# Two of x's eight transposed pieces: by TensorE, or by transposing DMAs with GpSimd's copies

## The chip, the cores and the metric

The kernel runs on one core of one Trainium2 chip. The metric is the device time of one execution in microseconds. The time before is 2468.52 us, the median of three runs (2468.34 to 2468.70).

## What is computed

Two transformer blocks of width 2048 run one after the other on one sequence of 256 tokens, all in f32. Only the very start of the first block matters here:

```
h    = rmsnorm(x, norm_attn)            # x is 256 x 2048
proj = h @ w_in                         # w_in is 2048 x 6144; q, k, v of two attentions
```

Everything behind it (two attentions, the output projection, a gated FFN, then a second block with a forgetting attention, an mLSTM, gates and a convolved FFN) is computed by the same kernel and is not touched.

## The kernel before, in words

**Products.** TensorE contracts over partitions, so `x` (tokens on partitions) has to be turned: `xT` has the 2048 features in 16 tiles (kt) of 128 partitions by 256 tokens. Each f32 operand is kept as a rounded part and a rest (`xT_hi`, `xT_lo`, `w_hi`, `w_lo`), and each product is three matmuls: hi by hi (line 623), hi by w_lo (624), lo by w_hi (625). The row norm's factor is applied later, when the sums leave PSUM.

**Units.** All the work on weights is one long series of units. A unit is 256 rows of a weight (two kt) by 512 columns: 12 matmuls of TensorE. SyncE's queue loads its 512 KB into `raw[n % 4]`, ScalarE makes `w_hi` (line 1042), VectorE makes `w_lo` (line 1449). There are four slots, so SyncE loads unit n when VectorE has split unit n - 4 (`lo_ready`), and ScalarE splits unit n + 4 when TensorE is done with unit n (`slot_used`). SyncE issues its loads one by one, in the order of the program: in stage `in_b`, three loads for each of units 1 to 7, four for each of units 8 to 15 (lines 502 and 505).

**The start.** The first group of 512 columns of stage `in_b` walks over all 16 kt in units 0 to 7, unit u needing kt 2u and 2u + 1. x comes in eight pieces of 256 columns, 256 KB each (`load_x`, line 444; pieces 6 and 7 are issued behind the weight loads of units 5 and 6). Piece j holds kt 2j and 2j + 1. For each piece:

- TensorE transposes its four 128x128 blocks into a PSUM bank (`start_T`, line 755; `start_more` waits for the piece and for the bank) and raises `kt_T`. Pieces 2 to 7 are turned behind units 0 to 5 (`behind` at line 826).
- ScalarE writes two tiles of `xT_hi` (`start_tile`, line 1066) and raises `kt_hi`; VectorE writes two tiles of `xT_lo` (`start_tiles`, line 1468) and raises `kt_lo`. For pieces 4 to 7 they do so right behind splitting the weights of units 4 to 7.
- TensorE waits ahead of unit u for `kt_lo` to reach 2u + 2 (`tiles_ready`, line 706).

Each engine works in the order of its program, so a wait in it holds all that stands behind it. ScalarE also sums squares of x for the norm (`half_squares`, line 1079), behind units' splits 1 to 4; GpSimd makes the norm's factor of them (line 2016 on), and before that it issues 14 small transfers (line 2007) and is then idle.

**The other way of turning, already used.** From the first attention head on, q and k (and much else) are turned without TensorE. A DMA can transpose 2-byte elements only, so GpSimd copies the f32 words apart into low and high halves (`halve_qk`, line 2049), SyncE issues a transposing DMA of 256 KB (`turn_heads`, line 454, at the units in `QK_ASKED`), and GpSimd joins the halves again into `qkT` (`join_turned`, line 2054). The same buffers serve this: `qk_bufs[1]`, `p_bufs[1]` and `qkT`, which are not in use during the first eight units.

Of the kernel before, what the change touches and what calls it, by code (L numbers as in the profile page):

```python
# [23 lines left out]
ACT = mybir.ActivationFunctionType  # L24
X = mybir.AxisListType.X
U16 = mybir.dt.uint16

P = 128
D = 2048
S = 256  # L30
NT = S // P
KT = D // P
# [14 lines left out]
NS = 4  # L47
# [13 lines left out]
G_ATTN, G_FFN, G_FINAL, G_NORM1, G_NORM2 = (KT * j for j in range(5))  # L61
# [53 lines left out]
START_BANKS = (4, 5, 6, 7, 2, 3, 4, 5)  # L115
# [57 lines left out]
            if 0 <= unit - HEAD_FIRST - k * HEAD_EVERY <= DIFF_STEPS[-1]]  # L173


QK_ASKED = {HEAD_FIRST + k_ * HEAD_EVERY + QK_SENT: k_ for k_ in range(2 * HEADS)}
QK_ASKED.update({PH["in_f"][0] + h_ * MLSTM_EVERY + 5: 2 * HEADS + h_ for h_ in range(M_HEADS)})
QK_ASKED.update({PH["gate_m"][0] + 12 * h_ + (4 if h_ else 6): 2 * HEADS + M_HEADS + h_ for h_ in range(4)})
QK_ASKED.update({PH["gate_a"][0] + 8 * h_ + (5 if h_ else 4): 2 * HEADS + M_HEADS + 4 + h_ for h_ in range(4)})
P_ASKED = {HEAD_FIRST + k_ * HEAD_EVERY + P_SENT: k_ for k_ in range(2 * HEADS)}  # L180
# [81 lines left out]
def two_blocks(nc, a, out):  # L262
    ctx = ExitStack()
    with ctx:
        def sb(name, shape, dt=F32):
            return ctx.enter_context(nc.sbuf_tensor(name, [P, *shape], dt))

        def sem(name):
            return ctx.enter_context(nc.semaphore(name))


        x = sb("x", [NT, D])
        xT_hi, xT_lo = sb("xT_hi", [KT * S], F32R), sb("xT_lo", [KT * S], F32R)
# [11 lines left out]
        gain = sb("gain", [N_GAIN])  # L285
# [20 lines left out]
        qkT = sb("qkT", [2, S])  # L306
# [21 lines left out]
        ps = [ctx.enter_context(nc.psum_tensor(f"ps{j}", [P, W], F32)) for j in range(8)]  # L328
# [21 lines left out]
        def across_bufs(buf, flipped_buf=None):  # L350
# [3 lines left out]
        qk_bufs = [across_bufs(z2[:, 0, C3 // 2:C3 // 2 + 4 * S]), across_bufs(z1[:, 0, 0:4 * S]),  # L354
                   across_bufs(tables), across_bufs(z2[:, 1, HALF:HALF + 2 * S], z2[:, 1, 2 * HALF:2 * HALF + 2 * S])]
        p_bufs = [across_bufs(z2[:, 1, C3 // 2:C3 // 2 + 4 * S]), across_bufs(z1[:, 1, 0:4 * S])]
        causal_bufs = [(split_[:, 0:3 * P].bitcast(U16).rearrange("p (e n) -> p e n", e=2), to[:, 0:3 * P].bitcast(U16).rearrange("p (e f s) -> p e f s", e=2, f=3))
                       for split_, to in ((work[:, 10 * S:12 * S], spare), *((z1f[:, c:c + 3 * P], z1f[:, c + 3 * P:c + 6 * P]) for c in (NT * (D + W), NT * D)))]
        y_split, y_flipped = (z2[:, 0, C3 - 2 * S + c * S:C3 - S + c * S].bitcast(U16).rearrange("p (t e n) -> p t e n", t=NT, e=2) for c in range(2))
        y_turned = z2[:, 1, C3 - 2 * S:C3 - S]  # L360
        qkT_halves = qkT[:, :, :].rearrange("p c s -> p (c s)").bitcast(U16).rearrange("p (f t s e) -> p f t s e", f=2, t=NT, e=2)
# [14 lines left out]
        x_landed = [sem(f"x_landed{j}") for j in range(4)]  # L376
# [4 lines left out]
        kt_T, kt_hi, kt_lo = sem("kt_T"), sem("kt_hi"), sem("kt_lo")  # L381
# [7 lines left out]
        halved, across, x_turned = sem("z_halved"), sem("z_across"), sem("x_turned")  # L389
        y_halved, y_across = sem("diff_y_halved"), sem("diff_y_across")  # L390
        m_halved, fox_joined = sem("mlstm_halved"), sem("fox_joined")
        qk_halved, qk_across, p_halved, p_across = sem("qk_halved"), sem("qk_across"), sem("p_halved"), sem("p_across")
        tanh_ready, silu_step, act_hi, act_lo = sem("tanh_ready"), sem("silu_step"), sem("act_hi"), sem("act_lo")
        conv_start, conv_step = sem("conv_start"), sem("conv_step")
# [40 lines left out]
        def _(sp):  # L435
# [9 lines left out]

            def turn_heads(unit):

                if unit in QK_ASKED:
                    k = QK_ASKED[unit]
                    sp.wait_ge(qk_halved, k + 1)  # L450
                    if 2 * HEADS <= k < 2 * HEADS + M_HEADS:
                        sp.wait_ge(m_halved, k + 1 - 2 * HEADS)
                    split_, flipped_ = qk_bufs[qk_buf(k)]
                    sp.dma_start_transpose(flipped_.rearrange("p t e f s -> p (t e f) s"),
                                           split_.rearrange("p t e n -> p (t e n)")).then_inc(qk_across, 16)
                if unit in Y_ASKED:
                    sp.wait_ge(y_halved, Y_ASKED[unit] + 1)
                    sp.dma_start_transpose(y_flipped.rearrange("p t e s -> p (t e) s"), y_split.rearrange("p t e n -> p (t e n)"))\
                      .then_inc(y_across, 16)
                if unit in P_ASKED:  # L460
                    k = P_ASKED[unit]
                    sp.wait_ge(p_halved, k + 1)
                    if k < 2 * HEADS:
                        split_, flipped_ = p_bufs[p_buf(k)]
                        to, of = flipped_.rearrange("p t e f s -> p (t e f) s"), split_.rearrange("p t e n -> p (t e n)")
                    else:
                        split_, flipped_ = causal_bufs[p_buf(k) - 2]
                        to, of = flipped_.rearrange("p e f s -> p (e f) s"), split_.rearrange("p e n -> p (e n)")
                    sp.dma_start_transpose(to, of).then_inc(p_across, 16)
# [100 lines left out]
            for i in range(2):  # L570
                for j in range(8):
                    n = PH["out_b"][0] + j
                    src, c = rows(w_out, HALF, D)[j % 4], (2 * i + j // 4) * W
# [42 lines left out]
        def _(pe):  # L616
# [207 lines left out]


            def behind(u):
                if u < 6:
                    start_more(2 + u)
                if u == 8:
                    small_T()  # L830
                if u in (10, 11):
                    pe.wait_ge(gain_ready, u - 8)
                heads(u)
# [196 lines left out]
        def _(act):  # L1030
# [31 lines left out]
            def start_tile(kt):  # L1062
                act.wait_ge(kt_T, kt // 2 + 1)
                if kt == 0:
                    act.wait_ge(gain_ready, 1)
                nc.scalar.activation(xT_hi[:, kt * S:(kt + 1) * S], ps[START_BANKS[kt // 2]][:, kt % 2 * S:(kt % 2 + 1) * S],
                                     ACT.Copy, scale=gain[:, G_ATTN + kt:G_ATTN + kt + 1]).then_inc(kt_hi, 1)
            for u in range(NS):
                if u == 1:
                    split(u, None, 0)  # L1070
# [5 lines left out]
            def half_squares(t, half):  # L1076

                c = slice(half * (D // 2), (half + 1) * (D // 2))
                nc.scalar.activation(sq_out0[:, t, c], x[:, t, c], ACT.Square, accum_out=half_ss[:, half, t:t + 1]).then_inc(x_sq, 1)
# [62 lines left out]
                        evac(name, i, g, z, (2 * i + g) * W, W, rstd)  # L1142

            def behind(u):
                if u < NS:
                    start_tile(2 * (NS + u))
                    start_tile(2 * (NS + u) + 1)
                if u in (1, 2):
                    half_squares(u - 1, 0)
                if u in (3, 4):  # L1150
                    half_squares(u - 3, 1)
                if u == 6:
                    act.wait_ge(rstd_ready, 1)
                if u == 9:
                    act.wait_ge(lam_step, 2)
                    nc.scalar.activation(lam_t[:, 2:4], lam_t[:, 0:2], ACT.Exp).then_inc(lam_exp, 1)
                heads_out(u, "in_b", 0, z1)
                heads(u)
# [281 lines left out]
        def _(dve):  # L1440
            v = nc.vector
# [22 lines left out]
            def start_tiles(u):  # L1464
                for kt in (2 * u, 2 * u + 1):
                    dve.wait_ge(kt_hi, 2 * u + 2)
                    c = slice(kt * S, (kt + 1) * S)
                    v.scalar_tensor_tensor(xT_lo[:, c], ps[START_BANKS[kt // 2]][:, kt % 2 * S:(kt % 2 + 1) * S],
                                           gain[:, G_ATTN + kt:G_ATTN + kt + 1], f32(xT_hi[:, c]), ALU.mult, ALU.subtract).then_inc(kt_lo, 1)
            dve.wait_ge(first_landed, 32)  # L1470
            v.tensor_copy(w_hi[0][:, 0, :], raw[0][:, 0, :]).then_inc(first_hi, 1)
# [105 lines left out]
                    (diff_head, dil_head)[kind](u, Head(0, head, 0))  # L1577

            def behind(u):
                if u < NS:  # L1580
                    start_tiles(NS + u)
                if u == 8:
                    parameters()
                if u == 9:
                    more_parameters()
                heads(u)
# [392 lines left out]
        def _(pool):  # L1979
            g_ = nc.gpsimd  # L1980
# [29 lines left out]
            def factor(n, dst):  # L2010
# [2 lines left out]
                pool.wait_ge(ms_ready, n)  # L2013
                return g_.tensor_tensor(dst[:], ms[:], minus_half[:, 0:NT], ALU.pow)

            pool.wait_ge(x_sq, 4)
            g_.tensor_tensor(ss[:], half_ss[:, 0, :], half_ss[:, 1, :], ALU.add).then_inc(x_sq, 1)
            pool.wait_ge(x_sq, 5)
# [37 lines left out]
            def join_qk(k):  # L2056

                s, head = (hb, ha)[k // HEADS], k % HEADS
                pool.wait_ge(hb.scores, 2 * min(k, HEADS))
                if k > HEADS:  # L2060
                    pool.wait_ge(ha.scores, head)
                join_turned(k).then_inc(s.qkT, 1)
# [284 lines left out]
```

## Time and profile before

| what | value |
|---|---|
| median of three runs | 2468.52 us (2468.34 to 2468.70) |
| the profiled execution's own time | 2468.15 us |
| its span in the profile | 2466.4 us |
| TensorE busy | 2460.6 us, 10974 matmuls |
| VectorE busy | 1497.7 us |
| ScalarE busy | 1208.0 us |
| GpSimd busy | 620.8 us |
| granted clock of TensorE | 1.0 over the span |

The span is the stretch between the first and the last instruction of the core; 1.75 us of the execution's time lie around it. Busy times of the engines overlap. In the rows below, L623 is line 623 of the kernel, PE is TensorE, PEld its weight loads, ACT ScalarE, DVE VectorE, POOL GpSimd and SPq the queue on which SyncE issues DMAs. Positions are microseconds from the span's start. A landing is counted from the start of the DMA's issue.

### The profile page before, as it was taken

To read this page: it belongs to the slowest core of one execution; us is meant where nothing else is said; L and a number is where in the kernel's file an instruction comes from. 1 tells how busy PE (TensorE), PEld (TensorE's weight loads), DVE (VectorE), ACT (ScalarE), POOL (GpSimd) and SP (SyncE) were. 2 spreads that over 40 slices of the span, in tenths; PEclk is the share of its full clock that TensorE was granted. 3 is DMA by queue.
4 is the path that set the end of the run, shared out by engine and by line. 5 is a ranking of instruction groups with operands and counts; after the bars stand their busy time and mean duration, and the time that the engine had idled before them with its cause. 6 is when DMAs were issued, how large, how long until landed. Compare 5 with 4: busy or idle time off the path is not lost.

```text
span 2466.4 us, 30149 instructions
## 1 busy us (share of the span) xinstructions
PE 2460.6 (100%) x10974; PEld 2037.7 (83%) x10974; DVE 1497.7 (61%) x1724; ACT 1208.0 (49%) x1622; POOL 620.8 (25%) x537
## 2 busy tenths in 40 slices
PE   9999999999999999999999999999999999999999
PEld 7888888888888888888888888888888888888887
DVE  5776666555455555565455555676567646675665
ACT  6555445444344434455444544544555545553553
POOL 2665524210012100131012322332334103320230
PEclk9999999999999999999999999999999999999999
DMA  9888868776677667687666677777777767876775
GB/s 251 214 204 213 207 195 228 210 204 201 192 204 208 202 195 201 201 242 205 177 205 201 191 204 202 209 214 223 220 217 203 219 192 220 219 208 195 202 227 178
DMA packets 491609, 511.80 MB, mean 208 GB/s; under 512 B 187136, under 2 KB 290020, under 8 KB 491360
## 3 DMA queue, kind: packets, MB, share of 16 engines
q1 hardware_dynamic: 489312, 507.36, 73.3%
q0 software_dynamic: 1088, 2.07, 0.3%
q8 instruction: 73, 1.20, 0.2%
q10 hardware_dynamic: 1088, 0.79, 0.1%
q14 instruction: 48, 0.39, 0.1%
HBM read 467.38 MB, written 2.11 MB: 190 GB/s over the span
## 4 chain that ended last, share of the span: by engine, by line
PE 99%; DMA 0%; ACT 0%; ACTq 0%; DVE 0%; issue 0%
PE ps L623 32%; PE ps L625 32%; PE ps L624 32%; PE ps L718 0%; PE ps L733 0%; PE ps L786 0%; PE ps L799 0%; DMA x<-in_x 0%; PE ps L975 0%; PE ps L755 0%; PE ps L658 0%; PE ps L952 0%; PE ps L907 0%; PE ps L906 0%; PE ps L640 0%; PE ps L645 0%
## 5 line engine op out<-in xcount | busy, mean ns | idle before, releaser
L1449 DVE TENSOR_TENSOR w_lo<-raw,w_hi 128x1024 fp32r<-128x1024 f32 x880 | 1152.2, 1312 | 921.8 <-ACT w_hi L1042 919.0
L1042 ACT ACTIVATE w_hi<-raw 128x1024 fp32r<-128x1024 f32 x879 | 929.4, 1059 | 1141.5 <-PE ps L625 1080.5
L623 PE MATMUL ps<-w_hi,xT_hi 128*128 128x512 f32 x2196 | 859.8, 392 | 0.0
L625 PE MATMUL ps<-w_hi,xT_lo 128*128 128x512 f32 x2196 | 854.9, 389 | 0.0
L624 PE MATMUL ps<-w_lo,xT_hi 128*128 128x512 f32 x2196 | 854.6, 389 | 0.0
L623 PE MATMUL ps<-w_hi,yT_hi 128*128 128x512 f32 x1312 | 511.0, 390 | 0.0
L625 PE MATMUL ps<-w_hi,yT_lo 128*128 128x512 f32 x1312 | 510.4, 389 | 0.0
L624 PE MATMUL ps<-w_lo,yT_hi 128*128 128x512 f32 x1312 | 510.4, 389 | 0.0
L623 PEld LDWEIGHTS ps<-w_hi,xT_hi 128*128 128x128 f32 x2196 | 412.3, 188 | 88.0 <-issue 2.5
L625 PEld LDWEIGHTS ps<-w_hi,xT_lo 128*128 128x128 f32 x2196 | 412.3, 188 | 85.8
L624 PEld LDWEIGHTS ps<-w_lo,xT_hi 128*128 128x128 f32 x2196 | 412.4, 188 | 85.0
L2138 POOL COPY work<-z 128x1024 uint16<-128x1024 uint16 x98 | 168.4, 1746 | 1046.7 <-DVE z L1679 543.2
L624 PEld LDWEIGHTS ps<-w_lo,yT_hi 128*128 128x128 f32 x1312 | 246.3, 188 | 51.1
L625 PEld LDWEIGHTS ps<-w_hi,yT_lo 128*128 128x128 f32 x1312 | 246.3, 188 | 51.1
L623 PEld LDWEIGHTS ps<-w_hi,yT_hi 128*128 128x128 f32 x1312 | 246.3, 188 | 50.9
L2143 POOL COPY work<-work 128x1024 uint16<-128x1024 uint16 x98 | 152.1, 1581 | 196.5 <-DMA work<-work 177.7
L1896 DVE SCALAR_TENSOR_TENSOR z<-work,conv,z 128x255 f32<-128x255 f32 (+1 forms) x176 | 74.7, 483 | 0.6
L1089 ACT ACTIVATE z<-ps,rstd 128x512 f32<-128x512 f32 x86 | 53.7, 675 | 0.0
L1391 ACT ACTIVATE z<-work,conv 128x256 f32<-128x256 f32 x88 | 45.4, 587 | 0.0
L2054 POOL COPY qkT<-z 128x1024 uint16<-128x1024 uint16 x20 | 29.6, 1479 | 36.7 <-DMA z<-z 36.7
L2068 POOL COPY z<-work 128x1024 uint16<-128x1024 uint16 x16 | 25.4, 1587 | 46.0 <-DVE work L1520 30.1
L1179 ACT ACTIVATE junk<-z 128x512 f32<-128x512 f32 x24 | 15.2, 635 | 31.4 <-DVE z L1628 31.0
(215 smaller groups left out, 924.7 us busy)
## 6 DMA issues: line engine op xcount, KB each, us to landing
raw<-in_w_up SPq DMA_DIRECT2D x264, 512.0 KB, 4.3
raw<-in_w_down SPq DMA_DIRECT2D x176, 512.0 KB, 4.4
raw<-in_w_in SPq DMA_DIRECT2D x160, 512.0 KB, 4.3
raw<-in_w_gate SPq DMA_DIRECT2D x88, 512.0 KB, 4.5
raw<-in_w_out SPq DMA_DIRECT2D x60, 512.0 KB, 4.6
raw<-in_w_in SPq DMA_DIRECT2D x191, 128.0 KB, 2.7
raw<-in_w_in SPq DMA_DIRECT2D x127, 192.0 KB, 3.1
raw<-in_w_proj_m SPq DMA_DIRECT2D x16, 512.0 KB, 4.0
```

What stands on the lines that cost most here:

```text
L623: pe.matmul(o, hi[:, q], w_hi[n % NS][:, k, 0:width], start=first, stop=False)
L624: pe.matmul(o, hi[:, q], w_lo[n % NS][:, k, 0:width], start=False, stop=False)
L625: mm = pe.matmul(o, lo[:, q], w_hi[n % NS][:, k, 0:width], start=False, stop=last)
L1042: nc.scalar.activation(w_hi[n % NS][:, :, 0:width], raw[n % NS][:, :, 0:width], ACT.Copy).then_inc(hi_ready, 1)
L1089: nc.scalar.activation(o, pair[g][t][:, 0:width], func, scale=scale[:, t:t + 1]).then_inc(by_act, 1)
L1391: nc.scalar.activation(z[:, f, :], turned[:, f, :], ACT.Identity, scale=conv[:, ds(col + 2 * CONV_T, 1)], bias=conv[:, ds(col + 3 * CONV_T ...
L1449: v.tensor_tensor(w_lo[n % NS][:, :, 0:width], raw[n % NS][:, :, 0:width], f32(w_hi[n % NS][:, :, 0:width]), ALU.subtract).then_inc(lo_rea ...
L1896: v.scalar_tensor_tensor(z[:, f, j:S], turned[:, f, 0:S - j], w, z[:, f, j:S], ALU.mult, ALU.add).then_inc(conv_step, 1)
L2054: return g_.tensor_copy(qkT_halves, qk_bufs[qk_buf(k)][1].rearrange("p t e f s -> p f t s e"))
L2068: g_.tensor_copy(p_bufs[k // HEADS][0], (mix_halves, prob_halves)[k // HEADS]).then_inc(p_halved, 1)
L2138: g_.tensor_copy(halves[:, t, :, :], z[:, t, :].bitcast(U16).rearrange("p (n e) -> p e n", e=2)).then_inc(halved, 1)
L2143: return g_.tensor_copy(turned_halves[:, c, :], flipped.rearrange("p e f s -> p (f s) e")[:, c, :])
```

## The change

Pieces 6 and 7 (`X_TURNED` = 6) go the other way:

- GpSimd waits for the two pieces and halves each into one buffer (`x_halved`), at the place where it otherwise waited for the sums of squares.
- SyncE issues the first transposing DMA behind the weight loads of unit 7 and the second behind those of unit 9 (`X_ASKED`). Ahead of the first it waits for the halving; ahead of the second also for `kt_T` 7, so for the first join.
- GpSimd joins piece 6 into `qkT` and raises `kt_T` to 7; then it joins piece 7 into the same `qkT`, when VectorE has read piece 6 out of it (`kt_lo` 14), and raises `kt_T` to 8.
- ScalarE and VectorE read these pieces from `qkT` in place of PSUM, and one unit later than before: piece 6 behind the split of unit 7, piece 7 behind that of unit 8. Pieces 4 and 5 keep their places.
- TensorE no longer transposes pieces 6 and 7 behind units 4 and 5.

```diff
+X_TURNED, X_ASKED = 6, {7: 0, 9: 1}
...
+        x_bufs = (qk_bufs[1], p_bufs[1])
...
             def turn_heads(unit):
 
+                if unit in X_ASKED:
+                    k = X_ASKED[unit]
+                    sp.wait_ge(x_halved, k + 1)
+                    if k:
+                        sp.wait_ge(kt_T, X_TURNED + k)
+                    split_, flipped_ = x_bufs[k]
+                    sp.dma_start_transpose(flipped_.rearrange("p t e f s -> p (t e f) s"),
+                                           split_.rearrange("p t e n -> p (t e n)")).then_inc(x_across, 16)
...
             def behind(u):
-                if u < 6:
+                if 2 + u < X_TURNED:
                     start_more(2 + u)
...
-                nc.scalar.activation(xT_hi[:, kt * S:(kt + 1) * S], ps[START_BANKS[kt // 2]][:, kt % 2 * S:(kt % 2 + 1) * S],
-                                     ACT.Copy, scale=gain[:, G_ATTN + kt:G_ATTN + kt + 1]).then_inc(kt_hi, 1)
+                src = ps[START_BANKS[kt // 2]][:, kt % 2 * S:(kt % 2 + 1) * S] if kt // 2 < X_TURNED else qkT[:, kt % 2, :]
+                nc.scalar.activation(xT_hi[:, kt * S:(kt + 1) * S], src, ACT.Copy, scale=gain[:, G_ATTN + kt:G_ATTN + kt + 1]).then_inc(kt_hi, 1)
...
             def behind(u):
-                if u < NS:
-                    start_tile(2 * (NS + u))
-                    start_tile(2 * (NS + u) + 1)
+                if u in (0, 1, 3, 4):
+                    j = NS + u - u // 3
+                    start_tile(2 * j)
+                    start_tile(2 * j + 1)
                 if u in (1, 2):
                     half_squares(u - 1, 0)
+                if u == 3:
+                    act.wait_ge(x_landed[2], 32)
+                    act.wait_ge(x_landed[3], 32)
...
-                if u < NS:
-                    start_tiles(NS + u)
+                if u in (0, 1, 3, 4):
+                    start_tiles(NS + u - u // 3)
...
+            for k in range(KT // 2 - X_TURNED):
+                j = X_TURNED + k
+                pool.wait_ge(x_landed[j % 4], 16 * (j // 4 + 1))
+                g_.tensor_copy(x_bufs[k][0], x[:, :, j * 2 * P:(j + 1) * 2 * P].bitcast(U16).rearrange("p t (n e) -> p t e n", e=2)).then_inc(x_halved, 1)
+            for k in range(KT // 2 - X_TURNED):
+                j = X_TURNED + k
+                pool.wait_ge(x_across, 16 * (k + 1))
+                pool.wait_ge(kt_T, j)
+                if k:
+                    pool.wait_ge(kt_lo, 2 * j)
+                g_.tensor_copy(qkT_halves, x_bufs[k][1].rearrange("p t e f s -> p f t s e")).then_inc(kt_T, 1)
             pool.wait_ge(x_sq, 4)
...
+                if k == 0:
+                    pool.wait_ge(kt_lo, KT)
```

VectorE's source in `start_tiles` (line 1468) changes as ScalarE's does. The last wait stands in `join_qk` (line 2056), ahead of the first head's join.

## Rows read from the trace of the kernel before

**Rows 1.** Page: busy time, chain by engine, ScalarE's weight splits (busy, mean | idle before)

```profile
PE 2460.6 (100%) x10974; PEld 2037.7 (83%) x10974; DVE 1497.7 (61%) x1724; ACT 1208.0 (49%) x1622; POOL 620.8 (25%) x537
...
PE 99%; DMA 0%; ACT 0%; ACTq 0%; DVE 0%; issue 0%
...
L1042 ACT ACTIVATE w_hi<-raw 128x1024 fp32r<-128x1024 f32 x879 | 929.4, 1059 | 1141.5 <-PE ps L625 1080.5
```

**Rows 2.** Waits of TensorE in the whole span: total us, times, longest

```profile
PE ps L766 <- POOL ones L1981: 1.1, 1, 1.1
PE ps L755 <- DMA x<-in_x: 0.7, 1, 0.7
PE ps L640 <- DVE w_hi L1471: 0.6, 1, 0.6
```

**Rows 3.** Timeline of TensorE, 17 to 31: start us, us, engine, line, operation

```profile
23.68 0.60 PE L755 MATMUL ps<-ident,x 128*128 128x128 f32 x4
24.03 0.48 PE L623 MATMUL ps<-w_hi,xT_hi 128*128 128x512 f32 x1
...
26.88 0.60 PE L755 MATMUL ps<-ident,x 128*128 128x128 f32 x4
27.23 0.48 PE L623 MATMUL ps<-w_hi,xT_hi 128*128 128x512 f32 x1
...
30.08 0.40 PE L623 MATMUL ps<-w_hi,xT_hi 128*128 128x512 f32 x1
```

**Rows 4.** Timeline of ScalarE, 14 to 36

```profile
26.77 1.06 ACT L1042 ACTIVATE w_hi<-raw 128x1024 fp32r<-128x1024 f32 x1 [0.57 <-DMA raw<-in_w_in]
27.73 0.82 ACT L1066 ACTIVATE xT_hi<-ps,gain 128x256 fp32r<-128x256 f32 x2
```

**Rows 5.** Timeline of VectorE, 14 to 33

```profile
27.86 1.23 DVE L1449 TENSOR_TENSOR w_lo<-raw,w_hi 128x1024 fp32r<-128x1024 f32 x1 [1.79 <-ACT w_hi L1042]
29.00 0.87 DVE L1468 SCALAR_TENSOR_TENSOR xT_lo<-ps,gain,xT_hi 128x256 fp32r<-128x256 f32 x2
```

**Rows 6.** Timeline of SyncE's queue, 14 to 36

```profile
14.34 0.46 SPq L444 DMA_DIRECT2D x<-in_x  x1
...
19.83 1.22 SPq L502 DMA_DIRECT2D raw<-in_w_in  x1
21.09 15.20 SPq L505 DMA_DIRECT2D raw<-in_w_in  x25
```

**Rows 7.** Line 444, 14.3 to 14.4: the load of piece 6, issue to landing

```profile
DMA to landing us min/median/max: 7.0/7.0/7.0
```

**Rows 8.** Line 505, 21.1 to 22.8: four weight loads (unit 8) and their landing

```profile
L505 SPq DMA_DIRECT2D raw<-in_w_in x4: 468/474/689, 21.1 to 22.6; - x4
...
DMA to landing us min/median/max: 4.3/4.4/5.9
```

**Rows 9.** Line 502, 19.7 to 20: unit 7's last load, issue to landing

```profile
DMA to landing us min/median/max: 6.9/6.9/6.9
```

**Rows 10.** Line 454 in the whole span: 256 KB transposing DMAs and their landing

```profile
L454 SPq DMA_TRANSPOSE z<-z x20: 1231/1232/2064, 45.1 to 1588.4; - x20
...
DMA to landing us min/median/max: 3.1/4.3/7.4
```

**Rows 11.** Timeline of GpSimd, 0 to 45: last small transfer and the next work

```profile
15.46 0.55 POOL L2007 DMA_DIRECT2D z<-in_conv_b  x1
31.72 0.19 POOL L2017 TENSOR_TENSOR ss<-half_ss 128x2 f32<-128x2 f32 x1 [15.72 <-ACT z L1079]
```

**Rows 12.** Lines 2049 and 2054: GpSimd's halving and joining copies; ns min/median/max

```profile
L2049 POOL COPY z<-work x16: 1036/1036/2015, 39.1 to 311.4; 128x1024 uint16<-128x1024 uint16 x16
...
L2054 POOL COPY qkT<-z x16: 1155/1298/2177, 48.7 to 321.5; 128x1024 uint16<-128x1024 uint16 x16
```

**Rows 13.** Timeline of TensorE, 0 to 12: the matmuls of ones

```profile
1.05 2.93 PE L766 MATMUL ps<-ones 128*128 128x128 f32 x12 [1.05 <-POOL ones L1981]
...
4.75 1.06 PE L766 MATMUL ps<-ones 128*128 128x128 f32 x8
```

More of the change, by code:

```diff
@@ L391, in two_blocks @@
         m_halved, fox_joined = sem("mlstm_halved"), sem("fox_joined")
+        x_halved, x_across = sem("x_halved"), sem("x_across")
         qk_halved, qk_across, p_halved, p_across = sem("qk_halved"), sem("qk_across"), sem("p_halved"), sem("p_across")
@@ L1467, in start_tiles @@
                     c = slice(kt * S, (kt + 1) * S)
-                    v.scalar_tensor_tensor(xT_lo[:, c], ps[START_BANKS[kt // 2]][:, kt % 2 * S:(kt % 2 + 1) * S],
+                    src = ps[START_BANKS[u]][:, kt % 2 * S:(kt % 2 + 1) * S] if u < X_TURNED else qkT[:, kt % 2, :]
+                    v.scalar_tensor_tensor(xT_lo[:, c], src,
                                            gain[:, G_ATTN + kt:G_ATTN + kt + 1], f32(xT_hi[:, c]), ALU.mult, ALU.subtract).then_inc(kt_lo, 1)
```

## The prediction, made before the changed kernel was run

> **What bounds the kernel now.** I read the page first: TensorE is busy 2460.6 us of the span of 2466.4, the chain that ended last is 99% TensorE, and ScalarE's splitting of the weights sits idle for over 1000 us waiting for TensorE [rows 1]. So weights are ahead, and nearly every microsecond that TensorE gains or loses is gained or lost for good. The waits of TensorE say whether a loss could be taken up later: they are three, 2.4 us in all, none behind the first ten microseconds [rows 2]. There is no slack behind the start. 0.2% of this time, 4.9 us, is about what a measurement of this kernel can tell from no change. Then I read the timelines of the five engines over the first 36 us, since the edit touches nothing else.
>
> **What it removes.** Two groups of four transposes leave TensorE. Unit 5 with the group behind it takes 27.23 - 24.03 = 3.20 us, unit 6 without one 30.08 - 27.23 = 2.85 [rows 3]: 0.35 each, 0.7 together. That is all that the edit can give, if everything else stays hidden: 2468.15 - 0.7 = 2467.45. Without these groups unit 5 would start at 24.03 - 0.35 = 23.68, unit 6 could start at 26.5, unit 7 at 29.4.
>
> **Where the tiles stand in ScalarE's and VectorE's order.** Piece 6 now comes behind the split of unit 7. That split waits for its weights and starts at 26.77; the two tiles behind it take 27.73 to 28.55 [rows 4]. VectorE splits unit 7 from 27.86 and does the two tiles from 29.00 to 29.87 [rows 5]. In the kernel before these places held piece 7, which unit 7 needs at 30.08, so they cost nothing. Now they hold piece 6, which unit 6 needs at 26.5. So even with piece 6 turned in time, unit 6 starts at 29.9: TensorE stands still for 3.4 us. Unit 7 could then start at 29.9 + 2.85 = 32.75, 2.7 us later than the 30.08 of before. This part is nearly certain.
>
> **Piece 6 on its way.** Its load is issued at 14.34 [rows 6] and lands 7.0 us later [rows 7], at 21.35. GpSimd is free by then: its last small transfer ends at 16.0 and it sat idle for 15.7 us until 31.72 [rows 11]. The halving isn't in the trace; its nearest row is the same copy for q and k, 1.04 us at the least and 2.0 at most [rows 12]. I take 1.2, since VectorE works beside it: 22.55. SyncE has issued unit 7's last load by 21.05 [rows 6], so its queue stands for 1.5 us. The issue itself holds the queue for 1.23 us [rows 10], until 23.8. The landing takes 3.1 to 7.4 us, in the median 4.3 [rows 10]; weight loads issued at 21 to 23 took 4.3 to 5.9 [rows 8]. I take 4.3, so 26.85; the join is 1.16 to 2.2, I take 1.3 [rows 12]: `kt_T` 7 stands at 28.15. ScalarE's place at 27.73 thus slips by 0.4, to 28.15 to 29.0, VectorE's tiles end about 29.9, and unit 6 starts at 30.0. Twenty transposing DMAs of a whole piece's size landed within 7.4 us each [rows 10]. The Trainium skill speaks against the edit: VectorE: DVE Perf Modes, The three transpose paths, gives a 128x128 transpose of 2-byte elements 390 ns on TensorE and 1309 ns by DMA, and tells to use TensorE where PSUM will do as the destination. A piece is eight such blocks; by that page, one after the other, they would be an estimated 10.5 us of DMA, and the two pieces would move the end by some 13 us more than my sum. The trace doesn't agree with eight in a row, so this gets no chance of its own.
>
> **Piece 7 on its way.** It is issued at 23.8 + the loads of units 8 and 9. These are eight issues; the queue's rate in rows is 0.47 to 0.69 us each when nothing holds it [rows 8], and 15.20 / 25 = 0.61 over a stretch with its waits [rows 6]. I take 0.55, so 28.2, which meets the other condition, `kt_T` 7 at 28.15. Issue at 28.2; by then the queue has been thin for a while, so I take the landing at 3.7, between the least and the median [rows 10]: 31.9. The join waits for `kt_lo` 14 (29.9, passed) and ends at 33.2. ScalarE's two tiles take 0.82 [rows 4], VectorE's 0.87 [rows 5], one behind the other since VectorE waits for both of ScalarE's: 34.9. Seven hand-overs of about 0.04 (unit 7's last load lands at 19.83 + 6.9 = 26.73 and its split starts at 26.77; VectorE follows ScalarE's end at 27.83 by 0.03 [rows 4, 5, 6, 9]) and rounding make 35.3. Unit 7 starts at 35.3 where it started at 30.08: **+5.2 us**. Halving of piece 7 lies in GpSimd's wait for the DMA and costs nothing; piece 7's load is issued ahead of unit 7's last, at 19.83 [rows 6], so with the same 7.0 it lands by 26.8 and is halved by 28.0.
>
> **What is queued behind the new waits.** On ScalarE, stuck ahead of piece 7's tiles: the last half of the squares and the splits of unit 9 on. Unit 9's split then ends at about 34.2 + 1.1 + 1.1 = 36.4, VectorE's at 37.7; TensorE wants unit 8 at 38.1 and unit 9 at 41, both are ready. On SyncE: two issues (2.5 us) and a stand of 1.5 us ahead of all loads from unit 8 on; unit 8's weights land near 30 and are split by 33. TensorE moves later by more than the queue does, so no load becomes late. On GpSimd: the norm's factor, wanted by ScalarE ahead of its first emptying of PSUM, which waits for unit 7 anyhow. I cost these at nothing; their cover is TensorE's own lateness.
>
> **The sum.** The own time of the profiled execution is 2468.15, 0.37 under the median. With +5.2 it is 2473.35, and against the median 2473.7 us, 0.21% more. The bounds of the unknown prices: with every one at its least (halving 1.04, issues of 0.49, landing 3.1, join 1.16) unit 7 starts at 33.8, +3.7; with halving 2.0, landings of 5.9 and 4.3, joins of 1.8 it is 39.2, +9.1.
>
> **The rivals.**
> 1. *Not slower by 0.2%.* SyncE's queue is the place: if halving, issue, eight loads, landing and join together take less than the 11.8 us that I gave them by 0.3 or more, the shift is under 4.9, down to 3.7, or 2.7 where only the order counts. For it: the least prices are near what an unhurried queue shows; against it: loads issued around 21 to 23 took 4.3 us and more [rows 8]. Time 2471.2 to 2473.4, about 2472.7. Chance 0.36.
> 2. *The clock falls.* TensorE stands for 3.5 us, works for 2.85, stands for 2.4. Its first 12 matmuls of ones took 2.93 us (0.24 each, the level of 1.2 GHz), the next eight 1.06 (0.13, the level of 2.4) [rows 13]; nothing in the trace stands so long behind that. If it falls, unit 6 takes 5.7, ends at 35.7, 0.4 past unit 7's tiles, and unit 7 may lose up to 2.85 in turn: +5.6 to +8.5, some 2475.5. Chance 0.10. The Trainium skill (TensorE: Matmul & The Clock Gate, Part 1) says that an idle TensorE falls back to half its rate and has to work to get it back, which is this rival.
> 3. *A late landing.* The first transposing DMA shares the queue's backlog: unit 7's last load took 6.9 us [rows 9]. With landings of 6 to 7 us `kt_T` 7 is late, the second issue waits for it, and the shift is +7 to +9: 2476.5. Chance 0.09.
> 4. *All hidden.* The gain of 0.7 stays, 2467.8. Against it stands the order on ScalarE; it needs unit 7's weights to land 3.4 us sooner than in the trace. Chance 0.02.
>
> **How the numbers follow.** The forecast, a shift of 4.9 to 7 by waiting for the second piece, has 0.43; it and rivals 2 and 3 are slower by over 0.2%: 0.62 less 0.01 for prices at the edge, 0.61. Rivals 1 and 4 are within 0.2%: 0.38. Faster by over 0.2% has no mechanism here; 0.01 is kept for what I overlook. The range goes from 2471.2, where the order alone counts, to 2478.0, the upper bound of the sum with a little of the clock's. The forecast's own range is 2473.4 to 2475.5.
>
> **What would show it.** In the changed kernel's timeline of TensorE: no line 755 behind unit 3; a stand from 26.5 to about 30 ahead of unit 6, released by VectorE's tile; another from 32.8 to about 35.3 ahead of unit 7; then no wait at all, and the total of waits up by 5 to 6 us. On SyncE a stand at 21.05 until 22.6. GpSimd: halvings at 21.4 and from about 24, joins ending near 28.2 and 33.3. I am wrong if unit 6 starts ahead of 29, if the second issue goes out well away from 28.2, if matmuls of unit 6 are 0.46 apart, or if the shift at unit 7 is right and the end differs.

## The result, and the profile after

The changed kernel takes **2474.29 us** in the median of 11 runs (2473.76 to 2475.07), the kernel before beside it 2468.38 (2468.07 to 2468.70, 11 runs): +5.9 us, a ratio of 1.0024 with a 95% interval of 1.0016 to 1.0032. The profiled execution is the run of 2475.07; it is compared with the 2468.15 of the profiled one before, +6.9. The rows come in the order of [rows 1 to 12].

The page, and below it the waits of TensorE (total, times, longest), changed kernel:

```profile
PE 2462.1 (100%) x10966; PEld 2037.8 (82%) x10966; DVE 1500.5 (61%) x1724; ACT 1208.4 (49%) x1622; POOL 631.6 (26%) x541
...
PE 98%; DMA 1%; SPq 1%; POOL 0%; issue 0%; DVE 0%; ACT 0%; POOLq 0%
```

```profile
PE ps L634 <- DVE xT_lo L1484: 4.4, 3, 3.6
PE ps L766 <- DMA x<-in_x: 1.7, 1, 1.7
PE ps L777 <- POOL ones L1997: 1.1, 1, 1.1
```

TensorE has eight matmuls fewer and is yet busy for 1.5 us more [rows 1]: something ran slowly. The second wait is for piece 1 and grew by 1.0 by chance (0.7 in [rows 2]; 0.7 to 1.3 in most profiles below). The first is new.

TensorE's timeline:

```profile
27.72 0.39 PE L636 MATMUL ps<-w_hi,xT_lo 128*128 128x512 f32 x1
31.66 0.80 PE L634 MATMUL ps<-w_hi,xT_hi 128*128 128x512 f32 x1 [3.56 <-DVE xT_lo L1484]
32.25 0.63 PE L635 MATMUL ps<-w_lo,xT_hi 128*128 128x512 f32 x1
32.68 0.63 PE L636 MATMUL ps<-w_hi,xT_lo 128*128 128x512 f32 x1
...
35.35 0.40 PE L634 MATMUL ps<-w_hi,xT_hi 128*128 128x512 f32 x1
35.59 0.40 PE L635 MATMUL ps<-w_lo,xT_hi 128*128 128x512 f32 x1
...
36.86 0.50 PE L634 MATMUL ps<-w_hi,xT_hi 128*128 128x512 f32 x1 [0.66 <-DVE xT_lo L1484]
```

Unit 6 starts at 31.66 after a stand of 3.56. Its first matmuls are 0.43 us apart, the last ones 0.24: TensorE's clock had fallen, and came back inside the unit. Unit 7 starts at 36.86 where it started at 30.08 [rows 3], 6.8 later. The windows of the same kernel show the clock (the column behind POOL's busy time is the granted share of full speed; 0.50 is 1.2 GHz):

```profile
28.00:32.00 4.00, 0.45 (x2) 0.34 (x2) 1.63 (x3) 2.21 (x5) 1.75 (x1) 0.94 0.90 222
32.00:36.00 4.00, 4.00 (x12) 2.97 (x11) 1.30 (x2) 1.69 (x4) 1.95 (x1) 0.63 0.88 228
36.00:50.00 14.00, 13.34 (x62) 10.89 (x62) 9.12 (x19) 8.32 (x11) 5.12 (x9) 1.00 0.72 207
```

The way of the two pieces, which [rows 4 to 6, 11] answer to: GpSimd, SyncE's queue, ScalarE and VectorE, one timeline each.

```profile
22.13 1.03 POOL L2035 COPY z<-x 128x1024 uint16<-128x1024 uint16 x1 [6.06 <-DMA x<-in_x]
24.98 1.04 POOL L2035 COPY z<-x 128x1024 uint16<-128x1024 uint16 x1 [1.82 <-DMA x<-in_x]
27.54 2.21 POOL L2042 COPY qkT<-z 128x1024 uint16<-128x1024 uint16 x1 [1.52 <-DMA z<-z]
33.01 1.95 POOL L2042 COPY qkT<-z 128x1024 uint16<-128x1024 uint16 x1 [3.25 <-DMA z<-z]
```

```profile
21.03 0.84 SPq L513 DMA_DIRECT2D raw<-in_w_in  x1
23.19 1.64 SPq L457 DMA_TRANSPOSE z<-z  x1
24.88 4.16 SPq L516 DMA_DIRECT2D raw<-in_w_in  x8
29.84 1.24 SPq L457 DMA_TRANSPOSE z<-z  x1
```

```profile
29.79 0.91 ACT L1078 ACTIVATE xT_hi<-qkT,gain 128x256 fp32r<-128x256 f32 x2 [2.30 <-POOL qkT L2042]
34.99 0.91 ACT L1078 ACTIVATE xT_hi<-qkT,gain 128x256 fp32r<-128x256 f32 x2 [2.31 <-POOL qkT L2042]
```

```profile
22.19 2.06 DVE L1464 TENSOR_TENSOR w_lo<-raw,w_hi 128x1024 fp32r<-128x1024 f32 x1 [1.76 <-ACT w_hi L1053]
27.52 1.23 DVE L1464 TENSOR_TENSOR w_lo<-raw,w_hi 128x1024 fp32r<-128x1024 f32 x1 [0.42 <-ACT w_hi L1053]
35.93 0.88 DVE L1484 SCALAR_TENSOR_TENSOR xT_lo<-qkT,gain,xT_hi 128x256 fp32r<-128x256 f32 x2 [1.99 <-ACT xT_hi L1078]
```

Line 457, the first and the second issue, to their landing:

```profile
DMA to landing us min/median/max: 4.3/4.3/4.3
...
DMA to landing us min/median/max: 3.1/3.1/3.1
```

Each hand-over is the one foretold: halving, issue, landing, join, `xT_hi`, `xT_lo`, unit. The join of piece 6 took 2.21 us. Ends are read off these rows by start plus duration: it ended at 29.75 and released the second issue at 29.84, though the queue had been free since 24.88 + 4.16 = 29.04.

### The profile page after: what moved, and what is told of

Its sections match the earlier page's. It is cut to its first block, busy times and chain, and to the rows that moved or that the text cites. A ratio compares the mean times of both kernels' runs of the same rounds, so it can differ in the third digit from the quotient of the medians.

```text
span 2473.3 us, 30141 instructions
## 1 busy us (share of the span) xinstructions
PE 2462.1 (100%) x10966; PEld 2037.8 (82%) x10966; DVE 1500.5 (61%) x1724; ACT 1208.4 (49%) x1622; POOL 631.6 (26%) x541
## 4 chain that ended last, share of the span: by engine, by line
PE 98%; DMA 1%; SPq 1%; POOL 0%; issue 0%; DVE 0%; ACT 0%; POOLq 0%
PE ps L634 32%; PE ps L636 32%; PE ps L635 32%; PE ps L729 0%; PE ps L744 0%; PE ps L797 0%; DMA z<-z 0%; PE ps L810 0%; DMA x<-in_x 0%; SPq L516 0%; PE ps L986 0%; SPq L513 0%; POOL qkT L2042 0%; PE ps L963 0%; SPq L447 0%; PE ps L918 0%
```

## The experiments

The kernels of one group ran on one chip, beside the kernel before; "+" is a median over that median. Beside it stands the profiled execution: where unit 7 starts, less the 30.08 of before, and its own time less 2468.15.

| kernel | median us | + | unit 7 | own time |
|---|---|---|---|---|
| again | 2474.35 | +6.0 | +6.9 | +7.1 |
| order_only | 2470.81 | +2.5 | +4.0 | +4.4 |
| gain_alone | 2468.16 | -0.2 | -0.2 | 0.0 |
| kept_busy | 2477.42 | +9.1 | +9.2 | +9.3 |
| kept_busy2 | 2474.29 | +5.8 | +6.4 | +6.6 |
| old_order | 2474.57 | +6.1 | +6.4 | +6.7 |
| side_work | 2469.49 | +1.0 | +0.9 | +1.8 |
| no_chain | 2472.88 | +4.4 | +5.9 | +6.2 |
| no_chain_busy | 2473.97 | +5.4 | +5.6 | +5.7 |
| join_alone | 2474.39 | +5.8 | +6.2 | +6.3 |
| no_chain_again | 2472.70 | +4.3 | +5.7 | +5.6 |
| no_chain_ones | 2472.23 | +3.9 | +3.9 | +4.0 |

(The kernel before had 2468.32 in the group of the first four, 2468.48 in that of kept_busy2 to no_chain, 2468.59 in that of the next two and 2468.38 in the last.) With one exception, side_work, a profiled run's own time moves by as much as the start of unit 7 does, within 0.4 us: what happens behind unit 7 adds little and gives nothing back. Where an expectation names a theory by a letter, the text below it says in words which held.

**again: the changed kernel, unaltered.**

> The changed kernel unaltered, as the measure for the others on the same chip. Theory A (TensorE waits for the tiles of piece 6 and then of piece 7): some 5.5 to 6 us above the kernel before, and in the profile a stand of 3 to 4 us ahead of unit 6 and a further one ahead of unit 7. In the first profile one microsecond of the 6.9 lay ahead of all this, in the landing of piece 1 (6.3 us where it had been 5.3). If that belongs to the change it is here again; if it is chance, unit 4 starts at the place it has in the kernel before and the shift is nearer 5.9.

2474.35 us (2473.40 to 2475.21, 10 runs), ratio 1.0024 (1.0015 to 1.0034): the result stands on another chip. All ten runs have a mean granted clock of 0.999, where the kernel before has 1.0 in 25 of its 26 (the other took 2470.68). In the profile here unit 6 took 5.2 us, from 31.79 to 36.97, and piece 7's tiles were done at 36.94: unit 7 followed at 36.99 without a wait.

**order_only: the kernel before, with the later places alone.** In ScalarE's program, and likewise in VectorE's:

```diff
-                if u < NS:
-                    start_tile(2 * (NS + u))
-                    start_tile(2 * (NS + u) + 1)
+                if u in (0, 1, 3, 4):
+                    j = NS + u - u // 3
+                    start_tile(2 * j)
+                    start_tile(2 * j + 1)
```

> The kernel before, with TensorE's transposes kept, and only the places of pieces 6 and 7 in ScalarE's and VectorE's order moved one unit later. Theory A: unit 6 can't start ahead of 29.9, unit 7 not ahead of 32.7, so the end is 2.7 us later (2.5 to 3.0), near 2471.1. Rival B (only the DMA route costs, the order lies in its shadow or costs nothing): within 0.3 us of the kernel before.

2470.81 us (2470.39 to 2472.50, 11 runs), ratio 1.0010 (1.0001 to 1.0019). TensorE's timeline and two windows of its profiled run, which is its slowest:

```profile
29.99 0.50 PE L623 MATMUL ps<-w_hi,xT_hi 128*128 128x512 f32 x1 [1.98 <-DVE xT_lo L1469]
...
31.50 0.63 PE L623 MATMUL ps<-w_hi,xT_hi 128*128 128x512 f32 x1
31.93 0.63 PE L624 MATMUL ps<-w_lo,xT_hi 128*128 128x512 f32 x1
...
34.49 0.57 PE L624 MATMUL ps<-w_lo,xT_hi 128*128 128x512 f32 x1
```

```profile
30.00:32.00 2.00, 2.00 (x8) 1.63 (x9) 1.36 (x2) 2.00 (x4) 0.00 (x0) 0.86 0.84 237
32.00:34.00 2.00, 2.00 (x6) 1.60 (x5) 1.30 (x3) 1.32 (x3) 1.11 (x3) 0.50 0.65 184
```

Unit 6 starts where the prediction had its floor, 29.9. The nine runs with a clock of 1.0 have a median of 2470.61, +2.3 where 2.7 was worked out. The two with 0.999 took 2472.13 and 2472.50, 1.7 more. So a stand of 2.0 us can bring the clock down, in some runs and not in others, and here nothing covers it.

**gain_alone: the removal, with nothing in its place.** TensorE leaves out the transposes of pieces 6 and 7 and no other engine makes them, so the last four kt of `xT` are made of what lies in those banks. ScalarE waits for the loads of those pieces itself.

```diff
-                if u < 6:
+                if u < 4:
                     start_more(2 + u)
...
-                act.wait_ge(kt_T, kt // 2 + 1)
+                act.wait_ge(kt_T, min(kt // 2 + 1, 6))
```

> The kernel before without the transposes of pieces 6 and 7 and with nothing in their place: ScalarE and VectorE read what is left in the banks, so the last four kt of xT are those of earlier pieces, and the output isn't the reference's. It gives the most that the change could have won. Theory A, from the rows: 0.7 us less than the kernel before (0.35 per group), 0.9 if the late first matmul behind each group counts too. Rival D (the transposes lay in a wait for weights or tiles): no difference.

2468.16 us (2467.74 to 2468.37, 11 runs), ratio 0.9998 (0.9989 to 1.0007): 0.16 gained, not 0.7, and the interval includes no change. TensorE's timeline shows where it went:

```profile
29.91 0.50 PE L623 MATMUL ps<-w_hi,xT_hi 128*128 128x512 f32 x1 [0.61 <-DVE xT_lo L1471]
```

Unit 7 waits 0.6 us for its tiles. VectorE starts them at 28.99 here and at 29.00 in [rows 5], whatever TensorE does, because they stand behind the split of unit 7's weights. In the kernel before they ended at 29.87, 0.2 ahead of unit 7. So the removal can give 0.2 at most, and this is the ceiling of the whole edit while the last tiles stand behind that split.

**kept_busy and kept_busy2: is the fall of the clock paid for?** Matmuls of ones ahead of units 6 and 7 of the changed kernel fill its stands; 30 and 14 in the first, 18 and 8 in the second.

```diff
+                if u in (5, 6):
+                    for _ in range((18, 8)[u - 5]):
+                        pe.matmul(ps[6][:, 0:P], ones[:], ones[:], start=True, stop=True)
                 if u == 8:
                     small_T()
```

> The changed kernel with 30 matmuls of ones (128 columns, result not read) ahead of unit 6 and 14 ahead of unit 7, so that TensorE doesn't stand and its clock shouldn't fall. In the changed kernel's profile seven matmuls of unit 6 were 0.43 us apart in place of 0.23, 1.4 to 1.6 us in all, and TensorE then still waited 0.66 us for piece 7. Theory A (the fall is covered, since unit 7 waits for piece 7's tiles anyhow): no shift against the changed kernel, within 0.4 us, and the stand ahead of unit 7 grows in place of the slow matmuls. Rival C (the clock is part of the loss): 1.3 to 1.6 us faster than the changed kernel.

> The changed kernel with fewer matmuls of ones than kept_busy, 18 ahead of unit 6 and 8 ahead of unit 7. A matmul of ones is two instructions of 0.113 us, so the 30 and 14 of kept_busy lasted 6.8 and 3.2 us, longer than the stands, and pushed unit 6 to 33.7; these last 4.1 and 1.8 us, shorter than the stands of 5.0 and (at full clock) 2.3. Theory A (the clock's fall is covered by the wait for piece 7): granted clock 1.0, unit 6 at full pace, and the end within 0.4 us of the changed kernel's 2474.35. Rival C (the fall is part of the loss): 1.3 to 1.6 us less, 2472.9.

kept_busy took 2477.42 us (2476.96 to 2478.38, 5 runs), ratio 1.0038 (1.0024 to 1.0051), and says nothing of the clock's price: I had sized it wrongly. Each call is two instructions of 0.11 us, so 30 of them lasted 6.9 us and held unit 6 themselves. kept_busy2, sized by that, took 2474.29 us (2474.07 to 2474.76, 10 runs), ratio 1.0023 (1.0013 to 1.0032), with a clock of 1.0 in every run. TensorE's timeline:

```profile
27.43 4.18 PE L842 MATMUL ps<-ones 128*128 128x128 f32 x36
...
34.19 1.95 PE L842 MATMUL ps<-ones 128*128 128x128 f32 x16
36.46 0.50 PE L634 MATMUL ps<-w_hi,xT_hi 128*128 128x512 f32 x1 [0.33 <-DVE xT_lo L1487]
```

With the clock kept up, unit 6 was done by 34.2 and unit 7 still waited for piece 7, until 36.46. The time is that of the changed kernel within 0.2 us. The clock falls in the changed kernel and costs nothing there that can be measured: the wait for piece 7 covers it, in the profile of again only just.

**old_order: the changed kernel with ScalarE's and VectorE's old places** (the diff of order_only, the other way round).

> The changed kernel with pieces 6 and 7 back at their old places in ScalarE's and VectorE's order, behind the splits of units 6 and 7. The order alone cost 2.3 us in runs whose clock stayed. Theory A says the two delays overlap and don't add: the join of piece 6 ends near 29.8, two microseconds behind ScalarE's later place, so the end stays within 0.5 us of the changed kernel's 2474.35. Rival E (they add): some 2.3 us less, 2472.0.

2474.57 us (2473.86 to 2476.12, 10 runs), ratio 1.0025 (1.0016 to 1.0034). Unit 6 started at 30.75, unit 7 at 36.51. Alone, the later places cost 2.3 us; taken out of the changed kernel they give nothing. The two delays lie beside one another.

**side_work: the kernel before, with the whole new route beside it, unused.** GpSimd, SyncE's queue and the DMAs do everything that the change gives them, the joined tiles are read by nobody, and TensorE's transposes serve.

```diff
+                if unit in X_ASKED:
+                    k = X_ASKED[unit]
+                    sp.wait_ge(x_halved, k + 1)
+                    if k:
+                        sp.wait_ge(x_joined, k)
...
+                g_.tensor_copy(qkT_halves, x_bufs[k][1].rearrange("p t e f s -> p f t s e")).then_inc(x_joined, 1)
```

> The kernel before, with TensorE's transposes and the old order in use, and beside it the whole new route run for nothing: halvings, both transposing DMAs at their places in SyncE's queue, both joins. It prices what is queued behind the new waits. Theory A: within 0.3 us of the kernel before, since weights are ahead by more than the 3 to 4 us by which the queue moves. Rival F: later weights or VectorE's splits, slowed beside GpSimd's copies (one took 2.1 us in place of 1.23 in the first profile), cost 0.5 to 2 us.

2469.49 us (2468.71 to 2469.94, 11 runs), ratio 1.0003 (0.9994 to 1.0012): +1.0. The interval includes no change, but even the fastest of these runs is above the median of the kernel before, 2468.48. Of the profiled run's +1.8, 0.6 stands ahead of the edit (TensorE starts piece 4's transposes at 17.63 where it did at 17.04). Some 0.3 more stands ahead of unit 7: VectorE's split of unit 7 took 2.16 us beside GpSimd's join (the rows are in the last section), so piece 7's tiles ended at 30.91 and the unit started at 30.98, where 0.23 behind its last matmul it would have been 30.67. ScalarE's and TensorE's timelines show what else:

```profile
35.71 1.06 ACT L1053 ACTIVATE w_hi<-raw 128x1024 fp32r<-128x1024 f32 x1 [2.40 <-DMA raw<-in_w_in]
38.02 1.06 ACT L1053 ACTIVATE w_hi<-raw 128x1024 fp32r<-128x1024 f32 x1 [1.25 <-DMA raw<-in_w_in]
...
42.60 1.06 ACT L1053 ACTIVATE w_hi<-raw 128x1024 fp32r<-128x1024 f32 x1 [1.42 <-DMA raw<-in_w_in]
```

```profile
43.11 0.50 PE L634 MATMUL ps<-w_hi,xT_hi 128*128 128x512 f32 x1 [0.48 <-DVE gain L1496]
```

The queue's two issues and their waits make the weights behind unit 7 late: ScalarE waits for their loads three times, where in the kernel before at most 0.66 us was waited for a load in that stretch. At 43.11 TensorE stands 0.5 us for VectorE's copy of later gains (`gain`), which stands in VectorE's order behind a split that is late with the loads. The other 0.4 of the 1.8 was not traced. The prediction put this at nothing, with TensorE's own lateness as the cover; with the cover gone the whole side work costs about 1.0.

**no_chain: the changed kernel, with the second transposing DMA asked for a unit sooner and joined into a buffer of its own**, so that it waits neither for the first join nor for VectorE.

```diff
-X_TURNED, X_ASKED = 6, {7: 0, 9: 1}
+X_TURNED, X_ASKED = 6, {7: 0, 8: 1}
...
-                    if k:
-                        sp.wait_ge(kt_T, X_TURNED + k)
...
-                if k:
-                    pool.wait_ge(kt_lo, 2 * j)
```

> The changed kernel without what makes piece 7 wait for piece 6: a second target buffer for the join and a semaphore of its own for the second DMA, which is asked behind the loads of unit 8 and waits for its halving alone. Its issue goes from 29.9 to about 27.1, piece 7's tiles from 37.0 to about 34.7. Theory A with the clock's fall: unit 6, started near 31.8 at half the clock, lasts until 36.1 to 36.9 and is now the bound itself, so the gain is 0 to 0.8 us: 2473.5 to 2474.3. Rival G (the clock is no bound): unit 7 starts at 34.7, 2.2 us less: 2472.2.

2472.88 us (2471.72 to 2474.33, 11 runs), ratio 1.0018 (1.0009 to 1.0027), 1.4 under kept_busy2 and 1.7 under old_order on the same chip, and between the two times expected (2473.5 to 2474.3 with the clock as the bound, 2472.2 without). The second issue went out at 27.30 and piece 7's tiles were ready at 34.0, but unit 7 started at 36.02: all of unit 6 ran at the lower clock. The cover of the clock's fall was gone. How much it costs was asked three times.

> no_chain with the 18 and 8 matmuls of ones of kept_busy2. In no_chain's profile piece 7's tiles were ready at 34.0, but unit 6 ran at half the clock from 30.73 and unit 7 started at 36.02. Theory A': the fall of the clock is covered while piece 7 comes late, and is the bound once it doesn't. Here unit 6 keeps its pace, the ones end near 35.3 at the latest, and the end is 0.8 to 1.6 us below no_chain's 2472.88, near 2471.7, where no_chain's one run with an undisturbed clock was. Rival H (the clock costs nothing here either): the same as no_chain within 0.4 us.

no_chain_busy has the 18 and 8 matmuls of ones of kept_busy2. 2473.97 us (2472.92 to 2474.72, 11 runs), where about 2471.7 was expected: a miss. Its tiles were ready at 34.6, but the second group of ones started at 34.02 and lasted 1.95, so it held unit 7 until 35.72. The next two ran side by side: no_chain unaltered, and no_chain with 18 matmuls of ones ahead of unit 6 alone.

> The version without the chain between the two pieces once more, unaltered, for a comparison on one chip with the next kernel. Both theories: about 1.5 us under the changed kernel, 4.4 above the kernel before; unit 6 runs at half pace all through and unit 7 starts near 36.0 although its tiles are ready near 34.0; granted clock 0.50 from 31 to 36.

> The same version with 18 matmuls of ones ahead of unit 6 alone and none ahead of unit 7, so that nothing added can hold unit 7. Theory A (without the wait for piece 7 as its cover, the fall of the clock costs real time): unit 6 starts near 31.2 at full pace, ends near 34.1, unit 7 starts with its tiles near 34.6, and the time is 1.0 to 1.5 us below the version without ones on the same chip. Theory G (the clock is not what holds the end there; the tiles and the later weights are): within 0.4 us of it. If the clock falls again in the short stand ahead of unit 7, the gain is smaller, 0.2 to 0.9, and the granted clock shows it from 34 on.

no_chain_again: 2472.70 us (2471.83 to 2473.97, 11 runs), ratio 1.0016 (1.0007 to 1.0025). no_chain_ones: 2472.23 (2471.34 to 2472.66, 11 runs), ratio 1.0015 (1.0006 to 1.0024). TensorE's timeline of no_chain_again, then of no_chain_ones:

```profile
30.75 0.80 PE L634 MATMUL ps<-w_hi,xT_hi 128*128 128x512 f32 x1 [4.23 <-DVE xT_lo L1484]
...
34.76 0.63 PE L634 MATMUL ps<-w_hi,xT_hi 128*128 128x512 f32 x1
...
35.73 0.39 PE L634 MATMUL ps<-w_hi,xT_hi 128*128 128x512 f32 x1
```

```profile
26.68 4.18 PE L842 MATMUL ps<-ones 128*128 128x128 f32 x36
30.79 0.50 PE L634 MATMUL ps<-w_hi,xT_hi 128*128 128x512 f32 x1
...
33.95 0.50 PE L634 MATMUL ps<-w_hi,xT_hi 128*128 128x512 f32 x1
```

Unit 6 starts at the same time in both, and unit 7 1.8 us earlier where the clock was kept up; the profiled runs differ by 2473.76 - 2472.11 = 1.65. The medians differ by only 0.5, where 1.0 to 1.5 was expected if the fall costs real time, and the two intervals overlap. The runs differ among themselves: the six of no_chain_again at 0.999 have a median of 2472.95, its five at 1.0 one of 2471.98, under the one with ones. So the fall costs 1.65 to 1.8 us where it hits in full and nothing covers it, by the two profiles, and some 0.5 in the median of this version, which is near the scatter of the runs.

**join_alone: the changed kernel, with VectorE's split of unit 7 behind piece 6's tiles**, so that nothing runs beside the join.

```diff
-            turn("in_b", 0, 16, behind)
+            for u in range(16):
+                if u == 3:
+                    behind(u)
+                split(NS + u, 0, 16)
+                if u != 3:
+                    behind(u)
```

> The changed kernel with one swap in VectorE's order: the split of unit 7 comes behind piece 6's tiles instead of ahead of them, so that it doesn't run beside GpSimd's first join. Where the two met, one of them took 2.1 to 2.2 us and the other its usual 1.15 or 1.23, in all profiles so far. Theory I (they share a way to the memory, and the join's length goes straight into the chain): first join 1.15 to 1.3 us, the split 1.23, both pieces 0.5 to 1 us earlier, the end 0.4 to 1.2 us below the changed kernel's 2474.35. Rival J (chance of the landings): joins as long as before and no change.

2474.39 us (2473.43 to 2476.05, 10 runs), ratio 1.0025 (1.0015 to 1.0034): no gain. GpSimd and the queue:

```profile
27.68 1.15 POOL L2047 COPY qkT<-z 128x1024 uint16<-128x1024 uint16 x1 [2.13 <-DMA z<-z]
33.18 1.15 POOL L2047 COPY qkT<-z 128x1024 uint16<-128x1024 uint16 x1 [4.35 <-DMA z<-z]
```

```profile
25.06 4.16 SPq L516 DMA_DIRECT2D raw<-in_w_in  x8
29.34 1.24 SPq L457 DMA_TRANSPOSE z<-z  x1
```

Both joins fell to 1.15 us, as the mechanism says, and the price I had given it was wrong. `kt_T` 7 now stood at 28.83, but the queue was busy with its eight loads until 29.22. The second issue left 0.5 us sooner than in the changed kernel, its landing took 3.8 instead of 3.1, and unit 7 started at 36.25. Behind the join stood the queue.

None of these versions beats the kernel before: the removal by itself gives 0.16 us, less than can be measured, and each way tried of making the two pieces elsewhere costs more. The old places together with no_chain's sooner second DMA were not tried.

## Why the prediction was right, and where its terms were off

The forecast held: slower by over 0.2%, by the wait for piece 7, inside the forecast's own range. Two of its own signs of being wrong showed all the same: the second issue went out 1.6 us later than foretold, and matmuls of unit 6 were 0.43 us apart. Term by term, against the profiled run of the changed kernel.

- **The removal, 0.7.** Over-valued: 0.16 (gain_alone). The step "unit 7 at 29.4" looked only at TensorE, and not at the tiles that end at 29.87 whatever it does. That row [rows 5] was in hand and used two paragraphs further down. Since the new waits hide it, the sum was not touched.
- **The order, a floor of 2.7.** Seen alone it is 2.3 (order_only), and in the changed kernel it doesn't bind: piece 6's own way ended later, so the old places give the same time (old_order). Right that the two are no sum.
- **Piece 6.** Landed and its halving begun at 22.13 (21.35 foretold; its issue was 0.8 late by the chance at the start), issue at 23.19 (22.55), of 1.64 us (1.23), landing 4.3 as foretold, join begun at 27.54 (26.85). Then the one step of the sum that was far off: the join at 1.3. It took **2.21**, so `kt_T` 7 stood at 29.75 and not at 28.15. The rows showed 1.16, a median of 1.3 and 2.2 [rows 12]; I took the median without asking what ran beside the long ones.
- **Piece 7.** Eight loads in 4.16 us, 0.52 each (0.55). Issue at 29.84 (28.2), landing 3.1 (3.7), join 1.95 (1.3), tiles and hand-overs 1.9 (2.1). Unit 7 at 36.86 (35.3), a shift of 6.8 for 5.2. The medians differ less, +5.9, since both profiled runs of this kernel were the slowest of theirs. Of the 0.7 that the median is over the forecast, join_alone shows that the join can't be all: without its delay the queue sets the same end.
- **The queue behind the waits, nothing.** Right with its cover, 1.0 without (side_work). Naming the cover was what made this testable.
- **The clock (rival 2).** Put at 0.10; it fell in all 21 runs of the changed kernel. The condition for its price was in the text: unit 6 at 5.7 us would end 0.4 past the tiles. But the clock came back inside the unit, so that it took 4.5 and ended at 36.2, under the cover; in the profile of again it took 5.2 and ended level with the tiles. That it cost nothing is in part luck: the cover had 0.6 us to spare in the one profile and nothing in the other. The chance of 0.10 for the fall was far too low. The Trainium skill (TensorE: Matmul & The Clock Gate, Part 1) says that an idle array falls to half its rate and must work to get it back; the trace agrees, with a granted clock of 0.63 from 32 to 36 and 1.00 from there on. What the prediction read off [rows 13] is a pace only: in the first 4 us of the kernel before the profile has a granted clock of 1.00, though the matmuls of ones are twice as far apart there.
- **A late landing (rival 3).** Not seen: 4.3 and 3.1 us for a whole piece, and 3.1 to 5.5 in all the profiles with this route. The Trainium skill (VectorE: DVE Perf Modes, The three transpose paths) has 1309 ns by DMA for a 128x128 block of 2-byte elements; by these rows, too, eight blocks are not turned one after the other at that figure, which would be an estimated 10.5 us.
- **Not slower by 0.2% (rival 1).** It was near: the interval of the ratio begins at 1.0016. no_chain, which takes one wait out of the chain, lies at 1.0018, under that bound.

## What to carry to other kernels

Ahead of taking work off the bounding engine, look at what comes ready next on the others: 0.7 us of TensorE was worth 0.16, since the next tiles stood 0.2 behind it. A route over another engine and a queue is a chain of hand-overs (here 7.6 us from piece 6's landing to `kt_T` 7, 22.13 to 29.75, for what TensorE does in 0.35), and shortening one link (the join, by 1.06 us) gives only what the link behind it leaves (0.5). A loss that is covered is not gone: the clock's fall and the side work behind the waits cost nothing in the changed kernel, and 0.5 to 1.8 us and about 1.0 where the cover was taken away.

## What the runs showed of the hardware

**GpSimd's copy and VectorE's split exclude one another.** Whichever of the two starts first runs at its own pace, and the other is held until it is done. Two pairs of the kernel side_work, GpSimd's timeline and then VectorE's:

```profile
27.89 1.17 POOL L2035 COPY qkT<-z 128x1024 uint16<-128x1024 uint16 x1 [2.41 <-DMA z<-z]
33.41 2.18 POOL L2035 COPY qkT<-z 128x1024 uint16<-128x1024 uint16 x1 [4.35 <-DMA z<-z]
```

```profile
27.97 2.16 DVE L1460 TENSOR_TENSOR w_lo<-raw,w_hi 128x1024 fp32r<-128x1024 f32 x1 [0.63 <-ACT w_hi L1053]
...
33.34 1.22 DVE L1460 TENSOR_TENSOR w_lo<-raw,w_hi 128x1024 fp32r<-128x1024 f32 x1 [1.07 <-ACT w_hi L1053]
```

First GpSimd is 0.08 ahead and VectorE takes 2.16 for what alone takes 1.23; then VectorE is 0.07 ahead and the join takes 2.18 for 1.15. Eighteen such pairs of a 128x1024 copy and a split, begun within 0.1 us of one another in the first 50 us of the profiles here, go the same way: eleven with GpSimd ahead (its copy 1.03 to 1.17, the split 2.04 to 2.22), seven with VectorE ahead (1.22 to 1.23, the copy 2.03 to 2.22). A few hundredths of a microsecond decide which engine pays about 1.0. The long copies of [rows 12] are such meetings too: of the 32 copies of the kernel before, the ten that took 1.4 us or more all began while VectorE ran a split, and the 22 of 1.04 to 1.16 did not. One of the ten, GpSimd's timeline and then VectorE's, kernel before:

```profile
221.91 2.02 POOL L2049 COPY z<-work 128x1024 uint16<-128x1024 uint16 x1
```

```profile
221.81 1.22 DVE L1449 TENSOR_TENSOR w_lo<-raw,w_hi 128x1024 fp32r<-128x1024 f32 x1 [1.36 <-ACT w_hi L1042]
```

The Trainium skill (SBUF — State Buffer, section "SBUF: two separate sides") says that a VectorE operation with two SBUF inputs and a GpSimd operation that reads SBUF share a pair of ports as an exclusive lock, the first to start keeping it for the whole instruction; the trace agrees in all eighteen, and join_alone, where its joins meet no split, has 1.15 twice.

**TensorE's clock falls in some runs and not in others of one kernel.** Behind a stand of 2.0 us it fell in 2 of 11 runs (order_only); with one of about 4.2 ahead of unit 6, 16 of the 22 runs of no_chain and no_chain_again show a mean of 0.999; with 3.6 and 5.0 in the profiles of the changed kernel, all 21 do. The kernel before shows 0.999 too, in 2 of the 98 runs beside the experiments; they took 2470.68 and 2471.18, 2.4 and 2.8 over their medians, and where the clock fell in them is not known. The run's own mean clock, a difference in the third decimal, told such runs apart, and was worth 1.0 to 1.7 us between the runs of one changed version. It is a coarse sign: over 2467 us a mean that rounds to 1.0 leaves room for an estimated 2.5 us at half the clock.
